# HGRN heads in a hybrid decoder step: diagonal chunk scores, earlier key transposes, quadrant inner products, one batch of outputs per head

## The reference

```python
def hgrn_chunked(q, k, v, log_f, s0):
    ...
    def step(s, inp):
        qc, kc, vc, lf = inp
        lc = jnp.cumsum(lf, axis=1)
        qt = qc * jnp.exp(lc)
        kt = kc * jnp.exp(-lc)
        a = jnp.where(tril, jnp.einsum('bchk,bshk->bhcs', qt, kt), 0.0)
        o = jnp.einsum('bhcs,bshv->bchv', a, vc) + jnp.einsum('bchk,bhkv->bchv', qt, s)
        lend = lc[:, -1]
        s = jnp.exp(lend)[..., None] * s + jnp.einsum('bshk,bshv->bhkv', kc * jnp.exp(lend[:, None] - lc), vc)
        return s, o
```

## Time and profile before

| | us |
|---|---|
| median of three runs | 2063.86 (2060.78 to 2070.21) |
| the profiled execution | 2063.47 |
| its span in the trace | 2061.6 |
| PE busy in the span | 2021.8 |

### The profile page before, as it was taken

The page is one execution under the profiler, slowest core; times in us unless marked ns, Lnnn a source line. Parts: engine busy times, 40 slices in busy tenths (PEclk is TensorE's granted clock), DMA queues, the critical chain, the costliest instruction groups (busy, mean ns, idle before and its releaser), DMA issues.

```text
span 2061.6 us, 34425 instructions
## 1 busy us (share of the span) xinstructions
PE 2021.8 (98%) x14058; PEld 1784.8 (87%) x14058; DVE 1295.3 (63%) x2262; ACT 743.2 (36%) x1432; POOL 308.6 (15%) x405
## 2 busy tenths in 40 slices
PE   8999999999999999999999999999999999999998
PEld 8997777769669999999899986898888888888896
DVE  3127777656642666767421426768888888888867
ACT  3127777755322443544221112132222222222323
POOL 0012000011410211311000000021113211122206
PEclk9999999999999999999999999999999999999999
DMA  9423010237661222222211114121111211111212
GB/s 217 127 68 129 12 42 12 93 127 252 236 197 48 58 58 48 69 54 61 65 52 42 52 61 133 41 82 42 41 52 42 63 50 41 41 52 42 62 41 83
DMA packets 140745, 159.12 MB, mean 77 GB/s; under 512 B 25842, under 2 KB 122443, under 8 KB 135724
## 3 DMA queue, kind: packets, MB, share of 16 engines
q1 hardware_dynamic: 132556, 114.14, 18.3%
q0 software_dynamic: 8032, 42.78, 6.7%
HBM read 141.32 MB, written 19.76 MB: 78 GB/s over the span
## 4 chain that ended last, share of the span: by engine, by line
PE 90%; DVE 4%; ACT 2%; SPq 1%; issue 1%; DMA 1%; POOL 0%; DVEq 0%; ACTq 0%; POOLq 0%
PE PS L1025 53%; PE PS L1791 12%; PE PS L1279 4%; PE PS L1367 3%; PE PS L1259 3%; PE PS L1686 2%; PE PS L1225 1%; PE PS L1352 1%; DVE arena L3002 1%; PE PS L1227 1%; PE PS L1594 1%; PE PS L1777 1%; PE PS L1288 1%; PE PS L1480 1%; PE PS L1537 1%
## 5 line engine op out<-in xcount | busy, mean ns | idle before, releaser
L1025 PE MATMUL PS<-x_low,w_high_mlp 128*128 128x344 f32 x1056 | 338.1, 320 | 0.0
L3002 DVE TENSOR_TENSOR arena<-arena,PS 128x512 f32<-128x512 f32 x336 | 225.0, 687 | 95.9 <-PE PS L1791 89.0
L1025 PE MATMUL PS<-x_high,w_low 128*128 128x344 f32 x768 | 246.3, 321 | 0.0
L1025 PE MATMUL PS<-x_high,w_high_mlp 128*128 128x344 f32 x720 | 231.6, 322 | 0.0
L1025 PEld LDWEIGHTS PS<-x_low,w_high_mlp 128*128 128x128 f32 x1056 | 198.5, 188 | 3.1
L1025 PE MATMUL PS<-x_low,w_high_hgrn 128*128 128x344 f32 x600 | 192.1, 320 | 0.0
L2149 ACT ACTIVATE aT<-PS 128x344 f32<-128x344 f32 x90 | 41.0, 455 | 372.8 <-PE PS L1025 314.0
L1791 PE MATMUL PS<-w_down_parts_high,hidden_parts_high 128*128 128x512 f32 x392 | 155.9, 398 | 1.0
L1791 PE MATMUL PS<-w_down_parts_high,hidden_parts_low 128*128 128x512 f32 x392 | 154.5, 394 | 0.0
L1025 PE MATMUL PS<-x_high_a,w_low 128*128 128x344 f32 x480 | 153.7, 320 | 0.0
L1025 PE MATMUL PS<-x_high_b,w_low 128*128 128x344 f32 x468 | 149.8, 320 | 0.0
(11 more groups left out here) (495 smaller groups left out, 4995.6 us busy)
## 6 DMA issues: line engine op xcount, KB each, us to landing
wring<-in_w_in SPq DMA_DIRECT2D x100, 256.0 KB, 3.4
wring<-in_w_up SPq DMA_DIRECT2D x64, 256.0 KB, 3.3
arena<-in_w_down SPq DMA_DIRECT2D x16, 1024.0 KB, 4.9
arena<-in_x_prompt SPq DMA_DIRECT2D x16, 512.0 KB, 3.6
x_high_kept<-x_high_att SPq DMA_DIRECT2D x1, 4128.0 KB, 14.0
arena<-in_w_out SPq DMA_DIRECT2D x2, 2048.0 KB, 8.6
out<-in_cache_win_kv SPq DMA_DIRECT2D x1, 4088.0 KB
out<-arena SPq DMA_DIRECT2D x7, 512.0 KB
```

The lines of the kernel that those rows point to most:

```text
L1025: mm = pe.matmul(out, w, x, start=(start and k == 0 and i == 0), stop=(stop and k == tiles - 1 and i == 2))
L3002: ins = dve.tensor_tensor(y, y, sums, ALU.subtract if m == 4 else ALU.add)
```

## The change

Five edits.

1. Scores: instead of one 128 by 128 product for each block of 128 tokens, four 32-column products, each for one chunk of 32 tokens, each into its own column group (output rows). The eight blocks take 32 products per head instead of 8. The mask becomes periodic, `atm` shrinks to 32 columns per block, and DVE copies each step with one `copy_predicated` instead of four.
2. Inner outputs: four products of 32 rows by 32 columns per block instead of one of 128 by 128.
3. All inner and all state outputs of a head stand together after k-tile 4 of the third chunk (after k-tile 3 in `merge_gate`).
4. The transposes of the keys of head h (h from 1 on) are issued right after k-tile 4 of the third chunk of the unit before, instead of behind the unit; the wait for `hk` moves with them. For head 7 that unit is `unit_g(3)`.
5. ACT copies the turned keys ahead of the third chunk of that unit.

```diff
-    put("hgmask", ((p[:, None] // CH == p[None, :] // CH) & (p[:, None] <= p[None, :])).astype(np.float32))
+    put("hgmask", (p[:, None] % CH <= p[None, :] % CH).astype(np.float32))
...
-        atm = view(o, NQ, P); o += NQ * P
+        atm = view(o, NQ, CH); o += NQ * P
...
                 if t == 0:
                     pe.wait_ge(*copied(wstep(h, 3)))
                     wbank(h, 8)
-                pe.matmul(PS[:, 3 + wstep(h, 8) % 5, DV * t:DV * (t + 1)], atm[:, t, :], vt[:, t, DV * h:DV * (h + 1)],
-                          start=(t == 0), stop=False, skip_group_check=True)
+                for j in range(4):
+                    rows = slice(CH * j, CH * (j + 1))
+                    pe.matmul(PS[rows, 3 + wstep(h, 8) % 5, DV * t:DV * (t + 1)], atm[rows, t, :], vt[rows, t, DV * h:DV * (h + 1)],
+                              start=(t == 0), stop=False, skip_group_check=True)
...
-            def unit_and_outputs(n, h):
+            def turn_decayed(h):
+                pe.wait_ge(hk, h + 1)
+                for s in (0, 1):
+                    bank = wbank(h, s)
+                    for j in range(4):
+                        t = 4 * s + j
+                        mm = pe.transpose(PS[:, bank, P * j:P * (j + 1)], lcb[:, P * t:P * (t + 1)], ident)
+                    mm.then_inc(w_ps, 1)
+
+            def unit_and_heads(n, h, turned=None):
...
-                        if ci == 1:
-                            out_inner(h, k)
-                        if ci == 2 and k in (1, 4):
-                            for t in range(4 * (k // 4), 4 * (k // 4) + 4):
+                        if ci == 2 and k == 4 and h is not None:
+                            for t in range(NQ):
+                                out_inner(h, t)
+                            for t in range(NQ):
                                 out_states(h, t)
+                        if ci == 2 and k == 4 and turned is not None:
+                            turn_decayed(turned)
 
             for h in range(HG):
                 if h and h % 2 == 0:
-                    unit_and_outputs(unit_f(h + 1), h - 1)
+                    unit_and_heads(unit_f(h + 1), h - 1, h)
+                elif h == 0:
+                    unit_matmuls(pe, unit_f(1))
+                    turn_decayed(0)
                 elif h + 1 < HG:
-                    unit_matmuls(pe, unit_f(h + 1))
-                pe.wait_ge(hk, h + 1)
-                for s in (0, 1):
...
+                    unit_and_heads(unit_f(h + 1), None, h)
                 for s in (2, 3):
                     bank = wbank(h, s)
                     for j in range(4):
-                        t = 4 * (s - 2) + j
-                        mm = pe.matmul(PS[:, bank, P * j:P * (j + 1)], kf[:, P * t:P * (t + 1)],
-                                       qT[:, h % 2, P * t:P * (t + 1)], start=True, stop=True)
+                        for a in range(4):
+                            c = 4 * (4 * (s - 2) + j) + a
+                            mm = pe.matmul(PS[CH * a:CH * (a + 1), bank, CH * j:CH * (j + 1)],
+                                           kf[:, CH * c:CH * (c + 1)], qT[:, h % 2, CH * c:CH * (c + 1)], start=True, stop=True)
                     mm.then_inc(w_ps, 1)
...
                 if h % 2 == 0:
-                    unit_and_outputs(unit_g(h // 2), h)
+                    unit_and_heads(unit_g(h // 2), h, HG - 1 if h == HG - 2 else None)
...
-                    if h is not None and k < 4:
...
+                    if h is not None and k == 3:
+                        for t in range(NQ):
+                            out_inner(h, t)
+                        for t in range(NQ):
+                            out_states(h, t)
...
-                    unit_copy(unit_f(h + 1))
+                    unit_copy(unit_f(h + 1), range(2 if h else 3))
+                    if h:
+                        for s in (0, 1):
+                            step_copy(h, s)
+                        unit_copy(unit_f(h + 1), (2,))
...
-                for s in (0, 1):
-                    step_copy(h, s)
+                if h == 0:
+                    for s in (0, 1):
+                        step_copy(h, s)
...
-                    unit_copy(unit_g(h // 2))
+                    unit_copy(unit_g(h // 2), range(2 if h == HG - 2 else 3))
+                    if h == HG - 2:
+                        for s in (0, 1):
+                            step_copy(HG - 1, s)
+                        unit_copy(unit_g(h // 2), (2,))
...
-                    for j in range(4):
-                        ins = dve.copy_predicated(atm[:, 4 * (s - 2) + j, :], maskb, PS[:, 3 + i % 5, P * j:P * (j + 1)])
-                    ins.then_inc(w_dve, 1)
+                    dve.copy_predicated(atm[:, 4 * (s - 2):4 * (s - 1), :].rearrange("p t c -> p (t c)"), maskb,
+                                        PS[:, 3 + i % 5, 0:P]).then_inc(w_dve, 1)
```

More of the change, by code:

```diff
@@ L1563, in unit_and_outputs @@
                             mm.then_inc(u_ps, 1)
-                        if ci == 1:
-                            out_inner(h, k)
-                        if ci == 2 and k in (1, 4):
-                            for t in range(4 * (k // 4), 4 * (k // 4) + 4):
+                        if ci == 2 and k == 4 and h is not None:
+                            for t in range(NQ):
+                                out_inner(h, t)
+                            for t in range(NQ):
                                 out_states(h, t)
+                        if ci == 2 and k == 4 and turned is not None:
+                            turn_decayed(turned)
             for h in range(HG):
                 if h and h % 2 == 0:
-                    unit_and_outputs(unit_f(h + 1), h - 1)
+                    unit_and_heads(unit_f(h + 1), h - 1, h)
+                elif h == 0:
+                    unit_matmuls(pe, unit_f(1))
+                    turn_decayed(0)
                 elif h + 1 < HG:
-                    unit_matmuls(pe, unit_f(h + 1))
-                pe.wait_ge(hk, h + 1)
-                for s in (0, 1):
-                    bank = wbank(h, s)
-                    for j in range(4):
-                        t = 4 * s + j
-                        mm = pe.transpose(PS[:, bank, P * j:P * (j + 1)], lcb[:, P * t:P * (t + 1)], ident)
-                    mm.then_inc(w_ps, 1)
+                    unit_and_heads(unit_f(h + 1), None, h)
                 for s in (2, 3):
@@ L1830, in _, with unit_copy @@
             split_high(act, 1, whA[:, 1])
-            def unit_copy(n):
+            def unit_copy(n, chunks=range(3)):
                 v, c, m, dst, fn = units[n]
-                for ci, (c0, cn) in enumerate(CHUNKS):
+                for ci in chunks:
+                    c0, cn = CHUNKS[ci]
                     act.wait_ge(u_ps, 3 * n + ci + 1)
```

## The result

The changed kernel takes 2042.06 us in the median of five runs (2041.56 to 2048.20), the kernel before beside it 2062.84 (2060.78 to 2070.21): ratio 0.9896, 95% interval 0.9876 to 0.9917. Measured a second time (experiment 8) the ratio was 0.9906, interval 0.9882 to 0.9930. The forecast was 2046.2 us, a gain of 17.3. The direction and most mechanisms are right, the size was put about 3 us too small, and the time stands at the lower edge of the stated range: 2042.06 just inside, the second median, 2041.91, just outside.

A forecast was written before the change was run, and what follows sets the result against it. PE was taken to bound the kernel. Outputs 8.8, scores 4.7, heads 2, 4, 6 1.3 and head 7 2.55 us sum to 17.3, so 2063.5 becomes 2046.2 us, range 2042 to 2060.

The forecast's parts named there:

- outputs, eight heads: Inner and state outputs in one batch of 2.26 us instead of 3.34 per head, saving 8.8 us for eight.
- first score to update, heads 0, 1, 3, 5: First score to first chunk update shortened by 1.17 us per head, 4.7 us for these four.
- heads 2, 4, 6: Chunk updates come 1.5 us earlier, 1.1 already counted under outputs: 0.4 us each, 1.3 us for three.
- head 7: Wait for ACT's copy of the turned keys disappears: 3.65 us, 1.1 already counted, so 2.55 us.
- outside the heads: PE is full behind the heads; no DMA or other engine there takes the gain back.
- Bound: PE, busy 98% of the span, bounds the kernel; whatever it gains in the heads arrives whole at the end.
- Rival (b): Inner quadrants take turns writing one bank: at 56 ns about 2065 us, or 2105 to 2110; chance 0.11.
- Scores: 32-column scores start 7.3 ns apart; DVE releases the first chunk update 0.87 us after the first score.
- Rival (a): Dense small instructions have a 27.7 ns floor: 2052.5 us with one new form, 2059.5 with both; chance 0.13.
- Early keys: Key transposes cost PE the same, about 0.9 us, inside the unit; ACT's copies ended the wait only in head 7.
- DVE's squares in heads 2, 4 and 6: DVE's chain from weight split to masked copy is the new bound there and hides 0.85 us of the gain.
- Rival (c): DVE binds more in heads 2, 4, 6, and the transposes wait 0.5 us each: 2.7 us, 2049; chance 0.08.

The follow-up runs named there:

- experiment 8: The changed kernel unaltered, measured again beside the kernel before: 2041.91 against 2061.78 us, ratio 0.9906; heads stretch 278.40 us.
- experiment 7: Changed kernel with all scores of a head in one step and one bank: 2041.56 us median, ratio 0.9904 to the kernel before; heads stretch 276.35 against 278.40 us.
- experiment 2: Kernel before with only the earlier key transposes and ACT's earlier copies: heads stretch 295.34 against 296.97 us; whole time 2058.10 us, executed once.
- experiment 4: Changed kernel with key transposes and ACT's copies back at their late places: heads stretch 289.28 against 278.56 us; whole time 2062.82 us, executed once.
- experiment 6: Changed kernel with DVE's square of a head's outputs issued twice: heads stretch 289.34 against 278.40 us; whole time 2055.74 us, executed once.
- experiment 3: Changed kernel with 128 by 128 scores and four masked copies per step again: heads stretch 289.88 against 278.56 us; whole time 2053.99 us, executed once.

## Why the prediction was right or wrong

The sum, term by term, by the ruler:

| term | forecast | measured |
|---|---|---|
| outputs, eight heads | 8.8 | 8.8 (3.35 to 2.25 us per head) |
| first score to update, heads 0, 1, 3, 5 | 4.7 | 4.1 |
| heads 2, 4, 6 | 1.3 | 3.0 |
| head 7 | 2.55 | 2.5 |
| heads together | 17.3 | 18.4 |
| outside the heads | 0 | 0.1, and 3.4 of clock scatter in the first pair of traces |

So the heads bring 1.1 us more than forecast: the forecast was 1.7 us too low for heads 2, 4 and 6 and 0.6 us too high for the scores of the other four, and the two errors partly cancel.

- **Bound.** Right: PE's microseconds arrive whole; the stretch behind the heads moved by 0.1 us.
- **Outputs.** Right: inner pitch 14.0 ns as taken from L1546; a batch of 2.25 us against a sum of 2.26. Rival (b), quadrants in turn, falls: four row groups wrote four quadrants of one bank at 14.0 ns. The rule of the Trainium skill on row tiles and banks ("TensorEngine Tiling (Array Packing)", "Gotcha 1: PSUM Pressure") does not hold in that form for outputs in different quadrants.
- **Scores.** Mechanism right (experiment 7), size 0.13 us too good per head: pitch 9.0 ns, not 7.3, and from DVE's start to the first update 0.45 us instead of about 0.38. Rival (a), a floor of 27.7 ns, falls, and with it the 25 ns of the Trainium skill's page "TensorE: Matmul & The Clock Gate" as a floor between different column groups.
- **Early keys.** Right that before they mattered in head 7 alone (experiment 2), and the order of PE was placed to 0.1 us (first score of head 2 at 29.10 us behind the updates of head 1, forecast 29.0). Costing them at nothing elsewhere was incomplete: experiment 4 shows that they carry 0.64 to 0.88 us in each of six more heads once the scores are short.
- **DVE's squares in heads 2, 4 and 6: the step that failed.** The term was 1.3 us for three heads, because I wrote that DVE would hide 0.85 us of the gain in each. The heads gave 3.0: DVE hid 0.25 in head 2 and 0.03 in the other two (in the second trace 0.03, 0.02 and 0.12). The chain from the weight split to the masked copy was forecast at 4.2 us and takes 3.46. The timeline of DVE of the changed kernel, head 2:

```profile
754.40 1.23 DVE L1049 TENSOR_TENSOR w_low<-wring,w_high_hgrn 128x1024 fp32r<-128x1024 f32 x1
755.54 0.69 DVE L2722 COPY arena<-PS 128x512 f32<-128x512 f32 x1
756.26 0.96 DVE L2724 TENSOR_TENSOR arena<-arena 128x512 f32<-128x512 f32 x1
757.26 0.69 DVE L2725 TENSOR_REDUCE arena<-arena 128x8 f32<-128x512 f32 x1
757.86 0.49 DVE L2745 COPY_PREDICATED arena<-consts_sb,PS 128x128 f32<-128x128 uint32 x2
```

  Two errors. The square was priced at the 1.44 us of one row and here took 0.96. That is 0.48 of the 0.72 us, and the 1.44 was no price of the square but held a wait for GpSimd (the last section has the figures). And I added 0.03 us between instructions of which two start 0.09 before the end of the one ahead: the other 0.24. The bound itself is real: experiment 6 made nearly all of an added 1.45 us of DVE arrive at PE. Rival (c), DVE binding harder, did not come; it bound less.
- **The base.** The sum was made against one profiled execution, 2063.47 us, which carried half clock at both places; the first trace of the changed kernel carried it at neither. The changed kernel's profiled execution, 2041.56, lies 4.6 us under the forecast: 3.4 are this, 1.1 the heads, 0.1 what lies behind them. The medians hold it less cleanly. The kernel before had 2062.84 and 2061.78 in the later runs, 0.6 and 1.7 under the base; with the 1.1 us of the heads that is at most 2.8 of the 4.1 us between 2046.2 and 2042.06, and the rest is scatter between executions. The range left no room below for that.

## What to carry to other kernels

When PE is full, small matmuls are worth gathering in one batch: a passage from full width into small tiles and back costs 0.33 us here whatever is inside, so the same quadrant products gain 5.7 us gathered, and woven in they make the heads stretch 1.9 us longer than before the change. Shortening one piece uncovers the copies that it had hidden, so an edit that is worth 1.6 us alone can be worth 7.7 beside another; ask of each wait what is second. A duration taken from one row may hold a wait for another engine: the square of 1.44 us takes 0.69 alone. And before a forecast is anchored to one profiled execution, look in its windows for stretches of lower clock outside the change.

## What was not expected of the hardware

- DVE's square (128x512) took 1.44 us before and 0.96 after in head 2, and it was GpSimd's product of the same size that stretched instead. GpSimd before and after:

```profile
762.99 1.04 POOL L3221 TENSOR_TENSOR consts_sb<-consts_sb,arena 128x512 f32<-128x512 f32 x1
```

```profile
756.07 0.61 POOL L3238 TENSOR_TENSOR vd_tail<-vd_tail,arena 128x256 f32<-128x256 f32 x1
756.64 1.49 POOL L3240 TENSOR_TENSOR consts_sb<-consts_sb,arena 128x512 f32<-128x512 f32 x1
```

  The starts tell who waits. Before, the square started at 763.14, behind GpSimd's product of 762.99, which ended at 764.03; the square ended at 764.58, 0.55 us later. After, it started at 756.26 behind a shorter GpSimd instruction, which ended at 756.68, and itself ended at 757.22, again 0.55 us later; now it was GpSimd's product that started second, and it ended 0.91 us behind the square. The traces of before, changed and experiments 6 and 8 hold 40 such squares. 34 started while a GpSimd instruction ran, and each ended 0.545 to 0.552 us after it; six started with none running, and each took 0.69 us. The second square of experiment 6 (1.42 us) is of the first kind. So in all 40 the square's own work is constant, and what varies is how long GpSimd's instruction still runs. No experiment moved the starts alone.
- Masked copies of 32 partitions by 128 elements took 2.48 us for eight, of 128 partitions by 128 elements 1.79 (experiment 3; the source of the former is also strided, and the two were not separated).
- The clock stayed full after the wait of 1.6 us in head 7 before and after five of six waits of 1.1 us in experiment 4. Half clock followed the sixth and the 2.7 us wait in head 7 of that experiment (some 1.5 us each), and two of three waits of 1.7 us in experiment 6 (3.1 us each). So a wait there can cost more than its own length, and its length alone doesn't tell which.
